# A triangle inverse by doubling: 64x64 blocks on two tiles of the array in place of 128x128 products

## The reference, cut to what matters

```
def step(state, inp):
    rt, wt, kt, vt, kkt, at = inp
    sa = jnp.einsum('bhvk,bhk->bhv', state, -kkt)
    state = state * wt[:, :, None, :] + sa[..., None] * (kkt * at)[:, :, None, :] + vt[..., None] * kt[:, :, None, :]
    return state, jnp.einsum('bhvk,bhk->bhv', state, rt)
```

## Time and profile before

| | us |
|---|---|
| median of the 3 runs | 1501.81 |
| lowest, highest | 1501.2, 1503.7 |
| span of the profiled execution | 1501.0 |
| TensorE matmuls busy | 1391.1 |
| VectorE, ScalarE, GpSimd busy | 792.6, 560.3, 622.7 |

### The profile page before, as it was taken

How to read it: one execution, slowest core, us unless ns; L and a number is a source line. 1 busy time by engine, 2 the same in 40 slices (tenths; PEclk the granted TensorE clock), 3 DMA queues, 4 the chain that set the end, 5 groups by cost and what they waited for, 6 DMA issues and landing times. The chain is left out here.

```text
span 1501.0 us, 24358 instructions
## 1 busy us (share of the span) xinstructions
PE 1391.1 (93%) x7722; PEld 1109.9 (74%) x7722; DVE 792.6 (53%) x1412; ACT 560.3 (37%) x1214; POOL 622.7 (41%) x584
## 2 busy tenths in 40 slices
PE   2999999999999999999999979899979999998995
PEld 1776877877878877868868857787757777776874
DVE  6546256365275374373373462207674747566457
ACT  3333344344244254244344353203242433335123
POOL 3643133242241350350251201577844636454872
PEclk9999999999999999999999989999979999999998
DMA  5211011011110120120120100333312212221331
GB/s 177 80 52 49 21 53 43 29 45 41 28 58 28 42 57 14 42 65 7 42 65 14 41 30 16 125 108 91 98 56 71 78 56 77 67 66 50 103 93 63
DMA packets 46687, 87.80 MB, mean 58 GB/s; under 512 B 5808, under 2 KB 6832, under 8 KB 46384
## 3 DMA queue, kind: packets, MB, share of 16 engines
q1 hardware_dynamic: 44352, 82.44, 18.5%
q10 hardware_dynamic: 2288, 4.72, 0.9%
HBM read 85.04 MB, written 2.10 MB: 58 GB/s over the span
## 5 line engine op out<-in xcount | busy, mean ns | idle before, releaser
L272 PE MATMUL psum<-h_split,w_hi 128*128 128x512 f32 x2320 | 754.5, 407 | 17.0 <-DVE h_split L1275 9.0
L255 POOL TENSOR_SCALAR w_hi<-w_raw 128x512 fp32r<-128x512 f32 x290 | 213.2, 735 | 828.1 <-PE psum L272 705.8
L272 PEld LDWEIGHTS psum<-h_split,w_hi 128*128 128x128 f32 x2320 | 438.9, 192 | 134.2 <-issue 37.8
L272 PE MATMUL psum<-mix 128*128 128x128 f32 (+4 forms) x3520 | 485.4, 292 | 19.2 <-ACT mix L831 7.0
L272 PE MATMUL psum<-h_split,w_lo 128*128 128x512 f32 x1160 | 458.8, 396 | 0.0
L272 PEld LDWEIGHTS psum<-mix 128*128 128x128 f32 (+1 forms) x3520 | 379.4, 176 | 89.5 <-issue 45.8
L257 POOL TENSOR_TENSOR w_lo<-w_raw,w_hi 128x512 fp32r<-128x512 f32 x290 | 410.5, 1416 | 24.2
L831 ACT ACTIVATE mix<-psum 128x256 f32<-128x256 f32 (+5 forms) x624 | 233.1, 391 | 459.8 <-PE psum L272 251.0
L272 PEld LDWEIGHTS psum<-h_split,w_lo 128*128 128x128 f32 x1160 | 222.1, 191 | 48.6
L1361 DVE COPY_PREDICATED mix<-mask,psum 128x128 f32<-128x128 uint8 (+2 forms) x312 | 135.6, 465 | 187.3 <-PE psum L272 184.3
L831 ACT ACTIVATE mix<-mix 128x512 f32<-128x512 f32 (+3 forms) x274 | 137.9, 538 | 158.9 <-DVE mix L1636 72.4
(11 more groups left out here) (118 smaller groups left out, 733.3 us busy)
## 6 DMA issues: line engine op xcount, KB each, us to landing
w_raw<-wall SPq DMA_DIRECT2D x290, 256.0 KB, 2.6
mix<-xT SPq DMA_DIRECT2D x4, 512.0 KB, 6.3
mix<-xT ACTq DMA_DIRECT2D x1, 2048.0 KB, 8.0
out<-mix SPq DMA_DIRECT2D x8, 256.0 KB, 2.1
mix<-mask_f SPq DMA_DIRECT2D x1, 1792.0 KB, 11.4
mix<-pT ACTq DMA_DIRECT2D x2, 512.0 KB, 3.5
mix<-lru_w ACTq DMA_DIRECT2D x4, 256.0 KB, 3.3
mix<-w2a ACTq DMA_DIRECT2D x16, 32.0 KB, 2.8
```

Of the source, the lines that this page charges most:

```text
L255: pool.tensor_scalar(w_hi[:, slot, :, :], w_raw[:, slot, :], 1.0, 0.0, ALU.mult, ALU.add).then_inc(sem["w_hi"], 1)
L272: return pe.matmul(o, lhsT, rhs, start=start, stop=stop, skip_group_check=True)
```

## The change

A chunk's 128x128 X and X' are kept as two diagonal 64x64 blocks (`quarters`: rows 0 to 63 and 64 to 127) up to level 5, in new buffers `xinv`, `zinv` and `p_half` of 64 columns for each chunk and head. `inv` is the full X', written by two ScalarE copies after level 5 and by VectorE at level 6. The chunks go in two groups of two (`g`). One step of P, N or T of a group is 8 products of 64x64 by 64 columns, alternately on rows and columns 0 to 63 and on rows and columns 64 to 127 of the array. T is no longer a transpose but a product with the identity. The copies from PSUM are as wide as before (128 or 256 columns) and do two chunks at once. A standalone increment of a new semaphore, `tile_groups`, stands ahead of each group of products and takes the waits. `inverse_start` stands behind `t(4)`, no longer between the products; `level_copies` stand within a level; `level 6` uses one 64x64 tile of the array for P and another for N. The reset of X' is one copy of 512 columns, a masked copy to the start of X' is split in two of 64 partitions, and at the start of the kernel `inv` is cleared too and `ident64` made.

```diff
-    rw_qk=8, rw_first=4, rw_masked=8, rw_init=4, rw_p=24, rw_pev=24, rw_n=24, rw_x=24, rw_t=20, rw_xt=20,
+    rw_qk=8, rw_first=2, rw_masked=8, rw_init=2, rw_p=12, rw_pev=12, rw_n=12, rw_x=12, rw_t=10, rw_xt=10,
...
-        inv = place(CH * T).rearrange("p (c s t) -> p c s t", c=CH, s=4)
-        p_full = place(4 * P).rearrange("p (r e t) -> p r e t", r=2, e=2)
+        inv = place(2 * CH * P).rearrange("p (c e t) -> p c e t", c=CH, e=2)
+        xinv, zinv, p_half = (place(T).rearrange("p (c e t) -> p c e t", c=CH, e=2) for _ in range(3))
+        ident64 = place(64)
...
+            quarters = [(64 * q, slice(64 * q, 64 * q + 64)) for q in range(2)]
+            def group_tiles(g):
+                for c in (2 * g, 2 * g + 1):
+                    for e in range(2):
+                        at = slice(((c % 2) * 2 + e) * 64, ((c % 2) * 2 + e) * 64 + 64)
+                        yield c, e, at
+            def inverse_start(r, g):
+                pe.wait_ge(sem["rw_masked"], count("rw_masked", r, 4 * g + 2))
...
+                pe.sem_inc(tile_groups, 1)
+                for c, e, at in group_tiles(g):
+                    for q, rows in quarters:
+                        last = mm(bank[2 + g][rows, at], zinv[rows, c, e, :], ident[rows, rows])
                 last.then_inc(sem["rw_first"], 1)
...
+            def inverse_p(r, lvl, g):
                 if lvl == 1:
+                    pe.wait_ge(sem["rw_masked"], count("rw_masked", r, 6 + g))
+                    pe.wait_ge(sem["rw_init"], count("rw_init", r, g))
                 else:
+                    pe.wait_ge(sem["rw_x"], count("rw_x", r, (lvl - 2) * 2 + g))
+                pe.sem_inc(tile_groups, 1)
+                for c, e, at in group_tiles(g):
                     if lvl < 6:
+                        for q, rows in quarters:
+                            last = mm(bank[4 + g][rows, at], rw_m[rows, c, e, 0, rows], xinv[rows, c, e, :])
                     else:
+                        last = mm(bank[4 + g][64:P, at], rw_m[0:64, c, e, 0, 64:P], xinv[0:64, c, e, :])
                 last.then_inc(sem["rw_p"], 1)
...
+            def inverse_n(r, lvl, g):
...
+                        for q, rows in quarters:
+                            last = mm(bank[6 + g][rows, at], zinv[rows, c, e, :], p_half[rows, c, e, :])
                     else:
+                        last = mm(bank[6 + g][0:64, at], p_half[64:P, c, e, :], inv[64:P, c, e, 64:P])
...
+            def inverse_t(r, lvl, g):
+                pe.wait_ge(sem["rw_x"], count("rw_x", r, (lvl - 1) * 2 + g))
+                pe.sem_inc(tile_groups, 1)
+                for c, e, at in group_tiles(g):
+                    for q, rows in quarters:
+                        last = mm(bank[2 + g][rows, at], xinv[rows, c, e, :], ident[rows, rows])
                 last.then_inc(sem["rw_t"], 1)
             def inverse(r, lvl):
                 inverse_p(r, lvl, 0)
                 if lvl > 1:
+                    inverse_t(r, lvl - 1, 1)
                 inverse_p(r, lvl, 1)
                 inverse_n(r, lvl, 0)
                 inverse_n(r, lvl, 1)
                 if lvl < 6:
                     inverse_t(r, lvl, 0)
...
                     for n in range(2 * CH):
                         product(r, n)
-                        if n >= 3 and n % 2:
-                            inverse_start(r, n // 2 - 1)
                     t(4, (1,))
-                    inverse_start(r, 3)
+                    for g in range(2):
+                        inverse_start(r, g)
...
+            def inverse(r, lvl, between):
                 inverse_p(r, lvl, 0)
                 if lvl > 1:
+                    inverse_t(r, lvl - 1, 1)
                 inverse_p(r, lvl, 1)
+                between()
                 if lvl < 6:
                     inverse_t(r, lvl, 0)
...
-                    for c in range(CH):
-                        last = f(inv[:, c, 2:4, :], fconst[:, 0:1, :].to_broadcast([P, 2, P]), ACT.Copy)
-                    last.then_inc(sem["rw_reset"], 1)
+                    f(zinv.rearrange("p c e t -> p (c e) t"), ident64.unsqueeze(1).to_broadcast([P, 2 * CH, 64]),
+                      ACT.Copy).then_inc(sem["rw_reset"], 1)
...
-            dve.memset(p_full, 0.0)
+            dve.memset(p_half, 0.0)
+            dve.memset(inv, 0.0)
...
-                            last = masked_copy(odd(inv[:, c, 2:4, :]), hg_mask[:, 0, 0:64].unsqueeze(1).to_broadcast([P, 2, 64]),
-                                               odd(by_head(bank[4])[:, :, 0, :]))
+                            for rows in quarters:
+                                at = slice(rows.start // 2, rows.stop // 2)
+                                last = masked_copy(odd(zinv[rows, c, :, :]), hg_mask[rows, 0, at].unsqueeze(1).to_broadcast([64, 2, 32]),
+                                                   odd(by_head(bank[4])[rows, :, 0, rows]))
```

More of the change, by code:

```diff
@@ L400, in inverse_n @@
                 if lvl >= 2:
-                    pe.wait_ge(sem["rw_xt"], count("rw_xt", r, n - CH))
-                o = bank[6 + c % 2]
-                for e in range(2):
+                    pe.wait_ge(sem["rw_xt"], count("rw_xt", r, (lvl - 2) * 2 + g))
+                pe.sem_inc(tile_groups, 1)
+                for c, e, at in group_tiles(g):
                     if lvl < 6:
-                        last = mm(o[:, e * P:(e + 1) * P], inv[:, c, 2 + e, :], p_full[:, c % 2, e, :])
+                        for q, rows in quarters:
+                            last = mm(bank[6 + g][rows, at], zinv[rows, c, e, :], p_half[rows, c, e, :])
@@ L462, in chain_u @@
                 for e, rows in heads:
-                    last = mm(R0[:, 64 + 64 * e:128 + 64 * e], inv[:, c, 2 + e, :], rhs_s[:, c % 2, rows])
+                    last = mm(R0[:, 64 + 64 * e:128 + 64 * e], inv[:, c, e, :], rhs_s[:, c % 2, rows])
                 last.then_inc(sem["rw_u"], 1)
@@ L945, in inverse_p @@
[L945 to L948 removed]
+                    even, _ = halves(flat(p_half[:, 2 * g:2 * g + 2, :, :]), 1 << lvl)
+                    src, _ = halves(bank[4 + g][:, 0:256], 1 << lvl)
+                else:
+                    even = flat(p_half[64:P, 2 * g:2 * g + 2, :, :])
+                    src = bank[4 + g][64:P, 0:256]
@@ L1042, in even_round @@
                 act.preload_act_table_set("natural_log_exp_and_others")
-                if pair:
-                    for c in range(CH - 1):
-                        inverse_start(r, c)
                 if head:
@@ L1051, in even_round, with copies @@
                 if pair:
-                    inverse_start(r, CH - 1)
+                    for g in range(2):
+                        inverse_start(r, g)
                 for lvl in range(1, 7):
+                    def copies(lvl=lvl):
+                        if head and lvl <= 3:
+                            level_copies(i, lvl)
                     if pair:
-                        inverse(r, lvl)
-                    if head and lvl <= 3:
-                        level_copies(i, lvl)
+                        inverse(r, lvl, copies)
+                    else:
+                        copies()
                 if pair:
@@ L1881 @@
         if lvl < 6:
-            pairs = (t[:, None] // (2 * m) == even[None] // (2 * m)) & (t[:, None] % (2 * m) >= m)
-            m8[:, 2816 + lvl * P:2816 + (lvl + 1) * P] = np.tile(pairs, (1, 2))
+            half = even[even < 64]
+            pairs = (t[:, None] % 64 // (2 * m) == half[None] // (2 * m)) & (t[:, None] % (2 * m) >= m)
+            m8[:, 2816 + lvl * P:2816 + (lvl + 1) * P] = np.tile(pairs, (1, 4))
     m8[:, 1792:2304] = np.tile(np.eye(P), (1, 4))
```

116 lines of the change are left out of this document (34 added, 82 removed).

## The result

The changed kernel takes 1513.7 us, the median of 5 runs (1508.2 to 1519.9), against 1501.81 for the kernel before: a ratio of 1.0082, with a 95% interval of 1.0061 to 1.0103. The forecast was 1455. The profiled execution has a span of 1514.1 us and a time of 1515.9 of its own.

A forecast was written before the change was run, and what follows sets the result against it. TensorE was taken to set the round's order, its inverse streaming products. The inverse saves 5.85 us a round, product steps cost 0.10: 8 rounds give 46 us off 1501.0, so 1455. Own range 1435 to 1475, overall up to 1490.

The forecast's parts named there:

- At nothing: Costed at zero: ScalarE's shorter reset copy (some 0.6 us), the start's memset of `inv` (about 1 us), the dropped `ru_u1`.
- What hides the rest: In the inverse, ScalarE's and VectorE's work stays under 3.14 us a level; GpSimd and weight loads make nothing late.
- Pair price: A small 64-column pair on two tiles in the inverse: 0.029 us, at most 0.058; 96 pairs are 2.8 us a level.
- Rival A: Row tiles writing one PSUM bank take turns in the inverse: groups of 0.93 us, 1553 us in all; chance 0.07.
- Handovers and level: Levels 2 to 5: 0.68 to 0.79 us from a group's stream to its dependent; 3.14 us a level, 0.34 idle.
- the entry: Start of the inverse, change of form, first group and P0's wait: 1.39 us, where one 0.22 stood.
- C: Copies, handovers and standalone increments bind the inverse: 3.7 to 4.1 us a level, 1480 to 1497 us; chance 0.14.
- D: The increment ahead of each group waits for an empty array: 0.82 us a group, 0.3 idle, 1535 us; chance 0.05.
- Level 1: First level of the inverse, without T1, T0 starting at 2.41 us: 2.88 us in all.
- Level 6: Last level of the inverse, P0 and P1 on one tile at 0.46 us each: 3.21 us to `chain_rhs`.
- rival B: TensorE's clock falls to 0.50 beneath the small products: a pair costs 0.058 us, about 1555 us; chance 0.04.
- The product steps: VectorE's small masked copy split in two costs 0.3 us in the loop, dropped transposes save 0.22: net 0.1 more.

The follow-up runs named there:

- after_flat: The changed kernel with TensorE's loop over the rounds written out, no branch back: 1493.36 us, ratio 0.9953 to the kernel before.
- after_wide145: The changed kernel with its loop, each group's 8 small products in levels 1, 4 and 5 replaced by one of 256 columns: 1470.24 us (one run).
- before_flat: The kernel before with TensorE's loop over the rounds written out, nothing else changed: 1499.88 us, ratio 0.9995.
- after_mix2: The changed kernel, loop written out, tile 5's products dealt out in eighths, six in the inverse between N0 and N1: 1466.47 us, ratio 0.9763 to the kernel before.

## Why the prediction was wrong

The step that failed is "At nothing". It went through the copy, the memset and a dropped semaphore, and under "What hides the rest" through ScalarE, VectorE, GpSimd and the weights, but never asked what brings TensorE its instructions. The change adds 56 pairs a level, 304 products and 304 loads a pass (983 and 981 where 679 and 677 stood), and the cost of their coming was set at nothing without a word. It has two parts.

- *The branch back.* The body went from 1526 to 2097 recorded instructions, past a limit between 1593 and 1705. Price: 19.9 us on five branches. `after_flat` took them away and gained 20 us.
- *The rate in the inverse.* A packet is 16 KB. In the old inverse a pair came each 0.111 us. At 0.029 us a pair the next block is late in part of the cases. Price in the round shown: levels 3 and 4 took 4.79 and 4.12 us, 2.63 more than twice 3.14. Of the 34.7 us in seven rounds, 9.6 are the clock's and 3 the other terms below; some 22 are left for the holes. `after_wide145`, without a fetch, has none of it.

The steps of the sum, measured in the round from 428 us where no hole falls into them:

- *Pair price.* 0.029 us, as taken. Rival A is refuted: tiles of different rows wrote one PSUM bank and their pairs didn't take turns. By the Trainium skill, "TensorEngine Tiling (Array Packing)", section Restrictions and Gotchas, they couldn't have; here the measurement decides against the page.
- *Handovers and level.* 3.14 us was forecast and 3.14 measured; the entry 1.39 and 1.35 (468.91 to 470.26). Rivals C and D are refuted with it. D's idle time ahead of every group isn't there: groups start 0.46 us apart.
- *Level 1.* 3.16 us where 2.88 was forecast. Half of that is the masked copy ahead of T0, which takes 0.44 us and not 0.30. The trace of the kernel before had this: its four copies of level 1 took 0.44 to 0.45, and the row that I costed from begins behind them, at 148.6 us.
- *Level 6.* 3.72 us where 3.21 was forecast. ScalarE had six copies back to back, since T1 of level 5 is two copies a group, and they stood ahead of P1's. I had costed one.

The last two show in the rows for VectorE in level 1, of the kernel before and of the changed one, and for ScalarE in level 6:

```profile
L1361 DVE COPY_PREDICATED mix<-mask,psum x4: 442/446/452, 144.1 to 146.8; 128x128 f32<-128x128 uint8 x4
```

```profile
472.34 0.91 DVE L1354 COPY_PREDICATED mix<-mask,psum 128x128 f32<-128x128 uint8 x2 [4.15 <-PE psum L274]
```

```profile
488.86 2.10 ACT L825 ACTIVATE mix<-psum 64x256 f32<-64x256 f32 x6 [1.47 <-PE psum L274]
```

- *The clock* (rival B). In the levels it stayed at 1.00. But it fell to 0.50 for 3.4 us behind some inverses and some branches; the two branch stretches of 16.70 and 18.23 us differ by that alone, 1.5 us. Fetches bring part of these falls, as the experiments show, and part comes without them; what sets them off isn't shown. They were no term of the sum.
- *The product steps.* 0.26 us a round, where 0.1 was taken.

For the round from 428 us this adds up. Holes 2.63, level 1 0.28, level 6 0.51 and the entry's -0.04 make 23.4 of 20.04; with the half clock's 1.6 behind it, and 0.3 less in the chain, the stretch is 28.34 where 29.47 - 5.85 = 23.62 was forecast. Without holes and at full clock it would be 24.1. That leaves 29.47 - 24.1 - 0.26 = 5.1 us a round for the change, 41 us in all instead of 46, an estimate of what it is worth when the instructions come for nothing.

The Trainium skill has the mechanism in "Runtime: NRT & Kernel Launch", section Instruction fetch mechanics: blocks of 16 KB or 256 instructions, fetched in sequence, and a stall at a taken branch whose target isn't there. The 16 KB, the 256 (253 recorded ones a packet) and the stalled branch agree with the traces. It calls the crossing of a block mostly hidden, which held for `before_flat` (0.9995) and not for pairs of 0.029 us. It gives TensorE room for 2048 instructions, and a body with 1705 recorded was fetched anew. Whether that figure is wrong stays open: the nine packets of such a pass hold some 2300 instructions, more than the body, and no run shows how much of the room is taken by what is fetched beyond it.

What stays open: why one packet has a hole behind it and the next has none, what makes the clock fall, and how much of `after_mix2`'s distance to 1455 is holes and how much the changes of form. Neither was tried by itself.

## What to carry to other kernels

Before cutting matmuls into small ones, count instructions as a resource: how many a loop body holds before and after, and how many the engine uses in a us. Look at the instruction queue on the page of the profile: a count of packets that would grow with the change is a warning, and "issue" waits in the middle of a group are its mark. Where the supply binds, try the loop written out (20 us here), and long products dealt in between the short ones (another 21 to 27). And take a copy's price from the level that it stands in.

## What was not expected of the hardware

- A taken branch on TensorE cost 0.21 us in the median with its body held (five kernels) and 3.3 to 3.8 us without (four kernels), and there was no case between: nine packets a pass at 1705 recorded instructions, none at 1593.
- Fetches were free for a slow user: 28 packets more in `before_flat` (59 for 31) changed nothing, while the holes in the changed inverse ended 2.3 and 2.7 us behind their packet.
- Two 64x64 tiles on different rows and columns wrote the same PSUM bank at 0.029 us a pair. The eight pairs of level 6 on one tile started 0.058 us apart, as taken, but from 488.44 us on, while the transpose group ahead of them was still starting its own (to 488.61): so they put off the next group by 0.3 us and not by 0.46.
- One product of 256 columns takes 0.43 us and the eight of 64 columns on two tiles 0.47, with an eighth of the instructions.
